# Seven block products in two more feed-forwards of a two-model kernel, and modulation units moved into down projections

## The chip, the cores and the metric

One core of one Trainium2 chip runs the whole program. The metric is the device time of one execution in microseconds (us); lower is better.

## The reference

Two models run one behind the other on 512 tokens of width 1024 (`D_MODEL`), in float32. The first has two layers, each a mixer and a SwiGLU feed-forward of width 2816; the second has one layer whose feed-forward has width 4096 and a squared ReLU. Shift, scale and gate of the first model's layers ("modulation") are one product of a condition vector with `ada_w` (1024 x 6144 in each layer).

```python
mod = cond @ ada_w[layer] + ada_b[layer]
sh1, sc1, g1, sh2, sc2, g2 = jnp.split(mod, 6, axis=-1)
...
h = modulate(rms_norm(x, ffn_norm[layer]), sh2, sc2)
x = x + g2[:, None, :] * swiglu(h, ffn_w1[layer], ffn_w2[layer])      # first model
...
u = jnp.square(jax.nn.relu(rms_norm_2(x, norm2_w) @ w_up))            # second model
return x + u @ w_down
```

## The kernel before, in words

Activations lie with features on the 128 partitions and the 512 tokens (`S`) along the free axis. Weights come as units of 128 x 1024 floats (512 KB), one for each 128 output features and 1024 inputs, from one long array `in_stream`. SyncE fills a ring of four (`ring`); GpSimd splits each unit into an upper half rounded to fp32r (`uppers`) and the rest (`lowers`, in the ring's own place). A plain product of one 128 x 128 weight block is three matmuls of 512 columns (upper by high, upper by low, lower by high; `products`), so a unit is 24 matmuls, here called a tile. Everything waits by semaphores, each engine runs its own program in order, and the order is written out by hand.

The stages are called m0 and f0 (mixer and feed-forward of layer 0), n1, m1 and f1 (layer 1), and f2 (feed-forward of the second model).

- **f0 before** (`ffn`): 44 up tiles in eleven rounds of four (gate, up, gate, up), the first round on the raw input before its norm is known, then 8 down tiles of 22 chunks each. VectorE multiplies gate by up, splits the result and writes it to `hid`.
- **f1 before** (`ffn1`): three plain rounds of four tiles, then 16 pairs of a gate and an up unit by **seven products**. A pair is seen as a 2 x 2 matrix of blocks (two units by two halves of the inputs) and the activations as 2 x 2 (halves of the inputs by halves of the tokens). Seven block products on sums of them (`seven_products`) take the place of eight: each is 4 x 3 matmuls of 256 columns, a pair 84 of them in place of 48 matmuls of 512. The sums and their halves are made beside it: VectorE `t_sum` and `t_lower`, ScalarE `t_upper`, `gate_uppers` and `up_uppers`, GpSimd one difference and four `lowers`; between products ScalarE copies partial results out of PSUM (`snaps`) and VectorE adds them back (`sums`). Since the sums need room, the hidden rows are kept only eight chunks at a time (`hid1`): the 22 chunks are taken in parts of 8, 8 and 6, each with its own down projection (`down_part`, stages f1a, f1b, f1c) and its own addition into the residual (`residual`).
- **f2 before**: two halves of 16 plain up tiles and 8 down tiles of 16 chunks.

**Modulation units.** `ada_w` is read in units of 128 x 1024, four to a group of 512 outputs. A unit is one DMA on ScalarE's queue into one of two buffers, and two multiply-adds of 128 x 512 on VectorE (`late_unit`, `ada_unit`); a group ends in `chunk_carry`, and TensorE sums it over the partitions with four small matmuls (`late_sum`, `ada_sum`), which wait until the fourth unit has been read. VectorE may overwrite `chunk_carry` only when that sum is done. Ten "late" groups are done in f0's up rounds: each round has one group, two units behind each pair, loaded into `sq` and `rs`. Four "last" groups are done in f0's down projection: VectorE takes group k ahead of `residual`'s chunk k, and TensorE sums group n-1 behind down tile n, for n = 1 to 4. TensorE may begin down tile n + 4 only when the residual of tile n has drained its bank.

Behind f0, `residual` with `held` makes the raw halves for n1 (`raw_split`, VectorE) for seven of eight chunks in one go, ahead of the last residual.

Of the kernel before, what the change touches and what calls it, by code (L numbers as in the profile page):

```python
# [38 lines left out]
P = 128  # L39
D = 1024  # L40
KC = D // P
# [97 lines left out]
def build(nc, A, plan):  # L139

    ctx = ExitStack()
    with ctx:
# [47 lines left out]
        late_w = [sq, rs]  # L190
# [27 lines left out]
        HIDDEN_AT = {"f0": 0, "f1": FF}  # L218
# [14 lines left out]

        PARTS = (KC, KC, FF - 2 * KC)
        HEAD = 2
        PLAIN = 3
# [63 lines left out]
        last_w = [big[:, TAIL + n * UNIT:TAIL + (n + 1) * UNIT].rearrange("p (a b) -> p a b", b=S) for n in (1, 2)]  # L300
# [105 lines left out]
        def _(pe):  # L406
# [370 lines left out]
            def late_sum(i):  # L777

                pe.wait_ge(sem("late_read1"), i * 2 + 2)
                for c in range(NT):  # L780
                    mm = pe.matmul(ps[:, 7, bass.ds(i * NT + c, 1)], C("chunk_carry")[:, c * P:(c + 1) * P],
                                   ones[:, 0:1], start=True, stop=True, skip_group_check=True)
                mm.then_inc(sem("late_sum_free"), 1)

            def ffn(st, layer):
                stream(f"w1_{layer}", 0, 2 * FF)
                slot = ring_loop(FF // 2, 4)
                take = bank_loop(FF // 2, range(4), [(st, "up", q) for q in range(4)])
                for q in range(4):
                    take(0, q)  # L790
                    raw_tile(st, q, q, slot(0, q), lambda k: (raw_hi[:, k, :], raw_lo[:, k, :]), True, loop["base"] + q)
                late_bank = nuse[7]
                uses["late"] = (7, late_bank)
                nuse[7] += 1
                with pe.Fori(1, FF // 2) as i:
                    for q in range(4):
                        take(i, q)
                        s = slot(i, q)
                        for k in range(KC):
                            if q == 0:  # L800
                                normed(st, k)
                            mm = products(ps[:, q, :], s, k, x_hi[:, k, :], x_lo[:, k, :], k == 0, k == KC - 1)
                        mm.then_inc(emptied[s], 1)
                    pe.wait_ge(drained[7], late_bank)
                    late_sum(i - 1)

                stream(f"w2_{layer}", 0, KC * FFU)
                slot = ring_loop(2, 4 * FFU)
                last_tile[st] = loop["base"] + (KC - 1) * FFU
                hidden = {FF - 2: (drained[1], nuse[1]), FF - 1: (drained[3], nuse[3])}  # L810
                take = bank_loop(2, range(4), [(st, "y", q) for q in range(4)], FFU)

                def down_tile(i, q):
                    take(i, q)
                    for f in range(FF):
                        if f % 8 == 0:
                            s = slot(i, FFU * q + f // 8)
                        if q == 0 and f in hidden:
                            pe.wait_ge(*hidden[f])
                        mm = products(ps[:, q, :], s, f % 8, hid[:, 0, f, :], hid[:, 1, f, :],  # L820
                                      f == 0, f == FF - 1)
                        if f % 8 == 7:
                            mm.then_inc(emptied[s], 1)
                    mm.then_inc(emptied[s], 1)

                for n in range(KC):
                    down_tile(n // 4, n % 4)
                    if 1 <= n <= ADA_LAST:
                        if n == 1:
                            claim(7, "late2", True)  # L830
                        ada_sum("last", n - 1, C("chunk_carry"), ps[:, 7, (n - 1) * NT:n * NT])
# [61 lines left out]
            def down_part(st, pack, part):  # L893
# [7 lines left out]
                with pe.Fori(0, 2) as i:  # L901
                    for q in range(4):
# [12 lines left out]
                        mm.then_inc(emptied[s], 1)  # L915

            def ffn1(st):

                stream("w1_1", 0, 2 * KC)
                slot = ring_loop(PLAIN, 4)  # L920
                take = bank_loop(PLAIN, range(4), [(st, "up", q) for q in range(4)])
                for q in range(4):
                    take(0, q)
                    raw_tile(st, q, q, slot(0, q), raw1, True, loop["base"] + q)
# [10 lines left out]
                down_part("f1a", "w2_1", 0)  # L935
                stream("w1_1", 2 * KC, 2 * KC)
                seven_products(st, KC)
                down_part("f1b", "w2_1", 1)
                stream("w1_1", 4 * KC, 2 * PARTS[2])
                seven_products(st, PARTS[2])  # L940
                claim(7, "meta_ss")
                pe.wait_ge(sem("meta_squared"), 1)
                for k in range(KC):
                    mm = pe.matmul(ps[:, 7, 0:META], ones[:, :], sq[:, 0, k * META:(k + 1) * META],
                                   start=k == 0, stop=k == KC - 1)
                mm.then_inc(full[7], 1)
                down_part("f1c", "w2_1", 2)
# [253 lines left out]
            ffn("f0", 0)  # L1201


            def late_raw(k):
                return late_hi[:, k, :], late_lo[:, k, :]

            stream("cd", 0, 4)
            raw_tiles("n1", [("u", t) for t in range(4)], late_raw, True)
# [13 lines left out]
            ffn1("f1")  # L1222
# [192 lines left out]
            for half in range(2):  # L1415
                st = f"f2{half}"
                stream("up2", half * HALF2, HALF2)
                slot = ring_loop(HALF2 // 4, 4)
                take = bank_loop(HALF2 // 4, range(4), [(st, "up", q) for q in range(4)])
                if half == 0:  # L1420
                    for q in range(4):
                        take(0, q)
                        raw_tile("f2", q, q, slot(0, q), x_halves, False)
                with pe.Fori(1 - half, HALF2 // 4) as i:
                    for q in range(4):
                        take(i, q)
                        s = slot(i, q)
                        for k in range(KC):
                            mm = products(ps[:, q, :], s, k, x_hi[:, k, :], x_lo[:, k, :], k == 0, k == KC - 1)
                        mm.then_inc(emptied[s], 1)  # L1430
                stream("down2", half * KC * 2, KC * 2)
                slot = ring_loop(2, 8)
                hidden = {HALF2 - 4 + b: (drained[b], nuse[b]) for b in range(4)}
                take = bank_loop(2, range(4), [(st, "y", q) for q in range(4)], 2)
                with pe.Fori(0, 2) as i:
                    for q in range(4):
                        take(i, q)
                        for f in range(HALF2):
                            if f % 8 == 0:
                                s = slot(i, 2 * q + f // 8)  # L1440
                            if q == 0 and f in hidden:
                                pe.wait_ge(*hidden[f])
# [56 lines left out]
        def _(act):  # L1499
# [66 lines left out]
            def ffn(st):  # L1566
                for m in range(2):
                    late_load(m, m)
# [1766 lines left out]
```

## Time and profile before

| | |
|---|---|
| median of 3 runs | 2526.47 us (2524.81 to 2528.64) |
| the profiled execution | 2526.73 us, its span 2524.7 us |
| PE busy | 2465.2 us, 98% of the span |
| POOL, DVE, ACT busy | 1787.9, 1144.8, 542.3 us |
| moved by DMA | 267.64 MB, mean 106 GB/s |
| mean granted TensorE clock | 0.992 |

In the profile PE is TensorE, DVE is VectorE, ACT is ScalarE, POOL is GpSimd, SP is SyncE; `ACTq` is ScalarE's sequencer, which issues its DMAs. A row names a line of the kernel, the engine, and output and inputs by the program's tile names. A matmul's duration is modelled and overlaps the next one's, so its pace is read from the distance of the starts.

### The profile page before, as it was taken

The page shows a single profiled execution, that of the slowest core. Times are in us where ns is not written, and L with a number is a line of the kernel's source. Part 1 is how long each engine was busy: PE and PEld are TensorE (multiplying, and loading weights), DVE is VectorE, ACT ScalarE, POOL GpSimd, SP SyncE. Part 2 cuts the span into 40 slices and gives each one's busy share as a digit, 9 for nine tenths or more (in the row PEclk, how much of TensorE's full clock was granted, in tenths as well). Part 3 has the DMA queues.
Part 4 walks back from the last instruction along what each step waited for, and adds up shares of the span by engine and source line. Part 5 has one row for each costly group of instructions (what it writes and reads, how often), then busy time and mean ns, then how long its engine had stood idle before and what let it go on. Part 6 is the DMA issues. An engine that isn't in the chain of part 4 may idle for free.

```text
span 2524.7 us, 34103 instructions
## 1 busy us (share of the span) xinstructions
PE 2465.2 (98%) x12183; PEld 1997.5 (79%) x12183; DVE 1144.8 (45%) x2070; ACT 542.3 (21%) x1091; POOL 1787.9 (71%) x1519
## 2 busy tenths in 40 slices
PE   6999999999999999999999999999999999999998
PEld 3677778888887768898988778788878888888886
DVE  5897756444337448363570223105664124331322
ACT  3213520000012522151511011113443101100100
POOL 5564367788887457767798755786555988888885
PEclk9999999999999999999999999999999999999999
DMA  6323225555532122232342211221112222222222
GB/s 260 125 75 134 75 100 178 188 182 173 195 104 75 47 68 92 99 109 93 107 159 97 84 59 59 84 92 67 59 51 101 93 98 92 93 98 100 92 100 83
DMA packets 73376, 267.64 MB, mean 106 GB/s; under 512 B 8240, under 2 KB 9024, under 8 KB 72768
## 3 DMA queue, kind: packets, MB, share of 16 engines
q1 hardware_dynamic: 60288, 215.97, 25.3%
q10 hardware_dynamic: 12992, 50.34, 5.8%
q8 instruction: 67, 1.10, 0.2%
q14 instruction: 29, 0.24, 0.0%
HBM read 262.08 MB, written 4.19 MB: 105 GB/s over the span
## 4 chain that ended last, share of the span: by engine, by line
PE 88%; DVE 6%; POOL 2%; ACT 1%; DMA 1%; issue 1%; ACTq 0%; DVEq 0%; SPq 0%; POOLq 0%
PE ps L444 22%; PE ps L445 22%; PE ps L446 22%; PE ps L845 2%; PE ps L849 2%; PE ps L848 2%; PE ps L675 2%; PE ps L676 2%; PE ps L677 2%; PE ps L1278 1%; PE ps L696 1%; PE ps L1334 1%; POOL lowers L2195 1%; DMA ring<-in_stream 1%; PE ps L1359 1%
## 5 line engine op out<-in xcount | busy, mean ns | idle before, releaser
L2192 POOL TENSOR_TENSOR uppers<-ring,ones 128x512 fp32r<-128x512 f32 x714 | 758.2, 1062 | 562.6 <-DMA ring<-in_stream 558.6
L2195 POOL TENSOR_TENSOR lowers<-ring,uppers 128x512 fp32r<-128x512 f32 x714 | 937.9, 1314 | 55.9
L444 PE MATMUL ps<-x_hi,uppers 128*128 128x512 f32 x864 | 351.5, 407 | 0.0
L446 PE MATMUL ps<-x_hi,lowers 128*128 128x512 f32 x864 | 337.3, 390 | 0.0
L445 PE MATMUL ps<-x_lo,uppers 128*128 128x512 f32 x864 | 337.0, 390 | 0.0
L444 PE MATMUL ps<-h_hi,uppers 128*128 128x264 f32 (+1 forms) x832 | 285.7, 343 | 4.0 <-DVE od_lo L3146 3.4
L445 PE MATMUL ps<-h_lo,uppers 128*128 128x264 f32 (+1 forms) x832 | 279.6, 336 | 0.0
L446 PE MATMUL ps<-h_hi,lowers 128*128 128x264 f32 (+1 forms) x832 | 278.8, 335 | 0.0
L445 PE MATMUL ps<-hid,uppers 128*128 128x512 f32 x704 | 274.3, 390 | 0.0
L444 PE MATMUL ps<-hid,uppers 128*128 128x512 f32 x672 | 263.0, 391 | 0.0
L446 PE MATMUL ps<-hid,lowers 128*128 128x512 f32 x672 | 261.6, 389 | 0.0
L1509 ACT ACTIVATE gate<-ps 128x512 f32<-128x512 f32 (+3 forms) x136 | 72.8, 536 | 731.1 <-PE ps L446 536.9
L444 PEld LDWEIGHTS ps<-x_hi,uppers 128*128 128x128 f32 x864 | 162.7, 188 | 42.6 <-issue 10.3
L445 PEld LDWEIGHTS ps<-x_lo,uppers 128*128 128x128 f32 x864 | 162.7, 188 | 38.6 <-issue 6.5
L446 PEld LDWEIGHTS ps<-x_hi,lowers 128*128 128x128 f32 x864 | 162.5, 188 | 34.8
L444 PEld LDWEIGHTS ps<-h_hi,uppers 128*128 128x128 f32 x832 | 157.2, 189 | 31.9 <-issue 8.8
L445 PEld LDWEIGHTS ps<-h_lo,uppers 128*128 128x128 f32 x832 | 157.2, 189 | 17.6 <-issue 0.7
L446 PEld LDWEIGHTS ps<-h_hi,lowers 128*128 128x128 f32 x832 | 157.1, 189 | 16.4
L445 PEld LDWEIGHTS ps<-hid,uppers 128*128 128x128 f32 x704 | 132.5, 188 | 27.7 <-issue 0.7
L1509 ACT ACTIVATE big<-ps 128x512 f32<-128x512 f32 (+7 forms) x151 | 68.0, 470 | 375.0 <-PE ps L446 184.8
L444 PEld LDWEIGHTS ps<-hid,uppers 128*128 128x128 f32 x672 | 126.2, 188 | 26.5 <-issue 0.5
L446 PEld LDWEIGHTS ps<-hid,lowers 128*128 128x128 f32 x672 | 126.1, 188 | 26.4
(432 smaller groups left out, 4180.9 us busy)
## 6 DMA issues: line engine op xcount, KB each, us to landing
ring<-in_stream SPq DMA_DIRECT2D x389, 512.0 KB, 3.2
sq<-in_ada_late ACTq DMA_DIRECT2D x20, 512.0 KB, 3.2
rs<-in_ada_late ACTq DMA_DIRECT2D x20, 512.0 KB, 4.7
big<-in_ada_late ACTq DMA_DIRECT2D x16, 512.0 KB, 4.3
big<-in_stream SPq DMA_DIRECT2D x13, 512.0 KB, 16.0
gate<-in_ada_rest ACTq DMA_DIRECT2D x12, 512.0 KB, 3.2
big<-in_ada_rest ACTq DMA_DIRECT2D x12, 512.0 KB, 3.8
hbuf<-in_stream SPq DMA_DIRECT2D x4, 512.0 KB, 6.8
```

The source lines that it names most:

```text
L444: pe.matmul(out, upper, hi, start=start, stop=False)
L445: pe.matmul(out, upper, lo, start=False, stop=False)
L446: return pe.matmul(out, lower, hi, start=False, stop=stop)
L675: pe.matmul(out, hi[:, at], upper, start=k == 0, stop=False)
L676: pe.matmul(out, hi[:, at], lower, start=False, stop=False)
L677: mm = pe.matmul(out, lo[:, at], upper, start=False, stop=k == KC - 1)
L845: mm = pe.matmul(out, upper[:, at], hi[:, k, :], start=start and k == 0, stop=False, skip_group_check=True)
L848: pe.matmul(out, upper[:, at], lo[:, k, :], start=False, stop=False, skip_group_check=True)
L849: mm = pe.matmul(out, lower[:, at], hi[:, k, :], start=False, stop=k == HALF_K - 1, skip_group_check=True)
L1509: return act.activation(out, in_, func, **kw)
L2192: pool.tensor_tensor(uppers[:, s, at], w[:, at], ones[:, 0:1].broadcast_to((P, UNIT // 2)), ALU.mult)\
L2195: pool.tensor_tensor(lowers[:, s, at], w[:, at], uppers[:, s, at].bitcast(F32), ALU.subtract)\
```

## The change

f0 now takes the way of f1, with its own ranges of units: three plain rounds, 2, 8 and 6 pairs by seven products, and three down parts (f0a, f0b, f0c). The modulation groups leave the up rounds. Late groups 0 to 4 go to f0a and 5 to 9 to f0b: VectorE does them between the residual's chunks, TensorE sums them behind down tiles 1, 2, 4, 5 and 6, and ScalarE issues their loads when its own part of the up run is done. The last four groups stay with the final down projection, which now is f0c with 6 chunks to a tile. The two load buffers are those of the last groups for all.

f2 takes two plain rounds (8 tiles), then 12 pairs by seven products, four to a run, each pair two up tiles with the squared ReLU (`wide_step`), and four down parts of 8 chunks.

```diff
-        late_w = [sq, rs]
...
+        LATE_GROUPS = ((0, 1), (2, 3, 4), (5, 6, 7, 8, 9))
+        LATE_SUM_BEHIND = (1, 2, 4, 5, 6)
...
+            def late_behind(n, first):
+
+                if n in LATE_SUM_BEHIND:
+                    late_sum(first + LATE_SUM_BEHIND.index(n))
+
+            def last_behind(n):
+
+                if 1 <= n <= ADA_LAST:
+                    if n == 1:
+                        claim(7, "late2", True)
+                    ada_sum("last", n - 1, C("chunk_carry"), ps[:, 7, (n - 1) * NT:n * NT])
...
+                down_part(st + "a", w2, 0, early)
...
+                down_part(st + "b", w2, 1, late)
...
+                down_part(st + "c", w2, 2, last)
...
+            def late_loads(first, count):
+
+                for unit in range(first, first + count):
+                    if unit >= 2:
+                        act.wait_ge(sem(f"late_read{unit % 2}"), unit // 2)
+                    late_load(unit, unit % 2)
+
...
                 for run in (1, 2):
+                    if st == "f0":
+                        late_loads(5 * ADA_UNITS * (run - 1), 5 * ADA_UNITS)
                     first_weights(st, run)
                     seven_run(st, run, 0)
...
+            def early_groups(k):
+
+                if k == 0:
+                    late_group(0)
+                    late_group(1)
+                    late_out(0)
+                elif 3 <= k < 6:
+                    late_group(k - 1)
+                elif k == 6:
+                    late_out(1)
+
+            def late_groups(k):
+
+                if k in (0, 1, 2, 4, 5):
+                    late_group(5 + (0, 1, 2, 4, 5).index(k))
+                elif k == 6:
+                    late_out(2)
...
-            residual("m0", "f0", 0, 2, raw=lambda k: (raw_hi[:, k, :], raw_lo[:, k, :]))
-            ffn("f0")
+            residual("m0", "f0", 0, 2, raw=raw0)
+            ffn1("f0", 0)
...
-            residual("f0", "n1", 0, 5, raw=lambda k: (late_hi[:, k, :], late_lo[:, k, :]), held=last_tile["f0"], last=True)
+            residual("f0c", "n1", 0, 5, raw=late0, held=True, last=True)
```

`late_out` waits on VectorE for the sums of the groups so far and adds the bias. ScalarE's step of a pair in f2 is that of f1 with these operations of its own:

```diff
+                act.wait_ge(sem("sums"), after(i, 10, 5 * (c + HEAD) + 3))
+                f(sq[:, 0, :], ps[:, 6, :], ACT.Relu).then_inc(sem("f2_relu"), 1)
+                act.wait_ge(sem("products"), after(i, 14, 7 * (c + HEAD) + 7))
+                f(gate[:, e, H:S], ps[:, 2 * e, 0:H], ACT.Relu).then_inc(sem("snaps"), 1)
+                act.wait_ge(sem("snaps"), after(i, 10, 5 * (c + HEAD) + 4))
+                link(f(sq[:, 1, :], gate[:, e, :], ACT.Square))
+                f(hid1[:, 0, first, :], sq[:, 1:2, :], ACT.Copy).then_inc(sem("f2_upper_half"), 1)
+                act.wait_ge(sem("sums"), after(i, 10, 5 * (c + HEAD) + 4))
+                f(hid1[:, 0, second, :], ps[:, 6:7, :], ACT.Copy).then_inc(sem("snaps"), 1)
```

**Where the late units stand on VectorE.** Of before, in one round of f0's up loop: two units (`big` is not among their inputs, `sq` and `rs` are) stand behind one pair's product and split.

```order
L2596 TENSOR_TENSOR ps<-gate,ps 128x512 [waits emptied2]
...
L2598 COPY hid<-ps 128x512
...
L2600 TENSOR_TENSOR hid<-ps,hid 128x512
...
L2417 TENSOR_SCALAR ps<-sq,cond 128x512 [waits late_filled0]
...
L2424 SCALAR_TENSOR_TENSOR ps<-sq,cond,ps 128x512 [waits late_half]
L2424 SCALAR_TENSOR_TENSOR ps<-rs,cond,ps 128x512 [waits late_read0,late_filled1]
```

Of the change, from the last step of f0's first up run to the first residual of f0a; `late_filled` is a landed unit, L2401 is the residual.

```order
L2538 TENSOR_TENSOR hid_62<-ps,hid_62 128x512 [waits snaps]
L2472 TENSOR_SCALAR ps<-big,cond 128x512 [waits late_filled0]
...
L2479 SCALAR_TENSOR_TENSOR ps<-big,cond,ps 128x512 [waits late_read0,late_filled1]
...
L2479 SCALAR_TENSOR_TENSOR consts<-big,cond,ps 128x512 [waits late_sum_free,late_half]
L2587 TENSOR_TENSOR mod<-ps,vecs 128x8 [waits late_sum_free]
L2401 SCALAR_TENSOR_TENSOR xres<-ps,mod,xres 128x512 [waits emptied1,drained7]
```

Before, two units stood behind each pair; now eight stand in a row with nothing between them, and twenty in each of f0a and f0b.

**Where TensorE waits for them.** Of the change, the end of tile 1 of f0a, the sum of late group 0 (L798), and the start of tile 2.

```order
L461 MATMUL ps<-hid_62,lowers 128x512
L798 MATMUL ps<-ones,consts 128x1 [waits late_read1,drained7]
L798 MATMUL ps<-ones,consts 128x1 x3
L459 MATMUL ps<-hid_62,uppers 128x512 [waits lower_made3,snaps,drained2]
L460 MATMUL ps<-hid_62,uppers 128x512
```

The sum stood behind four up tiles before, a whole round after the group's first load; now it stands behind the second down tile, with all of the part's later tiles queued behind it.

**Where the loads start on ScalarE.** Of the change, from ScalarE's last step of the first up run to the first loads.

```order
L1508 ACTIVATE gate<-ps 128x256 [waits products]
L1508 ACTIVATE hid1_62<-ps 128x512 [waits sums]
L1563 DMA big<-in_ada_late 128x1024 x2
L1563 DMA big<-in_ada_late 128x1024 [waits late_read0]
L1563 DMA big<-in_ada_late 128x1024 [waits late_read1]
```

The first two loads follow the run's last copy, and each later one waits until the unit two before it has been read.

## Rows read from the trace of the kernel before

**Rows 1.** The page: busy time; the chain that ended last, by engine.
```profile
PE 2465.2 (98%) x12183; PEld 1997.5 (79%) x12183; DVE 1144.8 (45%) x2070; ACT 542.3 (21%) x1091; POOL 1787.9 (71%) x1519
...
PE 88%; DVE 6%; POOL 2%; ACT 1%; DMA 1%; issue 1%; ACTq 0%; DVEq 0%; SPq 0%; POOLq 0%
```

**Rows 2.** Windows, PE alone: start:end, length, PE busy, clock, DMA share, GB/s.
```profile
389.30:616.40 227.10, 227.10 (x1042) 1.00 0.55 185
616.40:740.00 123.60, 123.60 (x562) 1.00 0.48 162
964.60:1008.20 43.60, 43.60 (x193) 1.00 0.29 97
1008.20:1029.30 21.10, 20.45 (x169) 1.00 0.29 101
1072.90:1154.10 81.20, 80.83 (x673) 1.00 0.31 104
1197.70:1258.80 61.10, 60.68 (x506) 1.00 0.31 103
```

**Rows 3.** PE's timeline: a late sum in f0; starts of two pairs in f1.
```profile
411.15 0.95 PE L781 MATMUL ps<-ones,consts 128*128 128x1 f32 x8
...
1093.62 0.28 PE L845 MATMUL ps<-x_hi,uppers 128*128 128x256 f32 x1
...
1103.70 0.28 PE L845 MATMUL ps<-x_hi,uppers 128*128 128x256 f32 x1
```

**Rows 4.** VectorE's timeline: the first group of four units in f0's down projection.
```profile
620.24 0.74 DVE L2394 TENSOR_SCALAR ps<-big,cond 128x512 f32<-128x512 f32 x1
...
625.45 1.55 DVE L2396 SCALAR_TENSOR_TENSOR ps<-big,cond,ps 128x512 f32<-128x512 f32 x2 [2.09 <-DMA big<-in_ada_late]
...
629.49 0.75 DVE L2400 SCALAR_TENSOR_TENSOR consts<-big,cond,ps 128x512 f32<-128x512 f32 x1
```

**Rows 5.** DMA issues of the page: KB each, median us to landing.
```profile
sq<-in_ada_late ACTq DMA_DIRECT2D x20, 512.0 KB, 3.2
...
big<-in_ada_late ACTq DMA_DIRECT2D x16, 512.0 KB, 4.3
```

**Rows 6.** Timeline of the next group: issues, then the two landings.
```profile
635.37 1.92 ACTq L1700 DMA_DIRECT2D big<-in_ada_late  x2
...
638.60 1.55 DVE L2396 SCALAR_TENSOR_TENSOR ps<-big,cond,ps 128x512 f32<-128x512 f32 x2 [1.67 <-DMA big<-in_ada_late]
642.22 0.76 DVE L2396 SCALAR_TENSOR_TENSOR ps<-big,cond,ps 128x512 f32<-128x512 f32 x1 [2.07 <-DMA big<-in_ada_late]
```

**Rows 7.** ScalarE's timeline: its last step of f1's first up run.
```profile
1030.72 0.60 ACT L1509 ACTIVATE hid<-ps 128x512 fp32r<-128x512 f32 x1 [0.83 <-DVE ps L2481]
```

**Rows 8.** VectorE's timeline: end of f0's down projection.
```profile
725.25 0.75 DVE L2348 SCALAR_TENSOR_TENSOR xres<-ps,mod,xres 128x512 f32<-128x512 f32 x1 [12.74 <-PE ps L446]
...
730.69 0.69 DVE L2307 CAST hid<-ps 128x512 fp32r<-128x512 f32 x1 [3.30 <-PE ps L446]
...
740.21 0.75 DVE L2348 SCALAR_TENSOR_TENSOR xres<-ps,mod,xres 128x512 f32<-128x512 f32 x1 [0.16 <-PE ps L446]
...
742.97 0.69 DVE L2308 TENSOR_TENSOR hid<-ps,hid 128x512 fp32r<-128x512 f32 x1
```

**Rows 9.** Windows, PE alone, around a wait of TensorE ahead of f1.
```profile
929.80:933.80 4.00, 0.04 (x2) 0.78 0.38 133
933.80:938.80 5.00, 5.00 (x20) 0.50 0.01 3
```

**Rows 10.** Timelines of ScalarE and VectorE between two pairs of f1.
```profile
1105.15 0.60 ACT L1509 ACTIVATE hid<-ps 128x512 f32 x1 [0.86 <-DVE ps L2481]
1105.64 0.38 ACT L1509 ACTIVATE rs<-ps 128x256 f32<-128x256 f32 x1
...
1106.61 0.69 DVE L2439 TENSOR_TENSOR ps<-ring 128x512 f32<-128x512 f32 x1
1107.21 0.42 DVE L2465 TENSOR_TENSOR gate<-ps,rs 128x256 f32<-128x256 f32 x1
```

More of the change, by code:

```diff
@@ L783, in late_sum @@
                 mm.then_inc(sem("late_sum_free"), 1)
[L785 to L831, printed above, removed]
@@ L900, in down_part, with tile @@
                 done = state["pairs"]
-                with pe.Fori(0, 2) as i:
-                    for q in range(4):
+                def tile(i, q, first=True):
                         take(i, q)
@@ L1412, in _, with wide_part @@
             mix_out("m2", "w_out2", lambda k: (od_hi[:, k, :], od_lo[:, k, 0:S]))
[L1415 to L1434, printed above, removed]
+            def wide_part(seg):
+                st = f"f2{seg}"
+                for t in range(KC):
+                    stream("down2", (seg // 2) * 2 * KC + 2 * t + seg % 2, 1)
+                slot = ring_loop(2, 4)
+                plain = {KC - 4 + b: (drained[b], nuse[b]) for b in range(4)}
+                take = bank_loop(2, range(4), [(st, "y", q) for q in range(4)])
+                done = state["pairs"]
                 with pe.Fori(0, 2) as i:
@@ L2321, in sum_square, with residual @@
                 ins.then_inc(sem("x_summed"), 1)
-            def residual(y, st, layer=None, part=0, raw=None, held=None, rs2=False, last=False, between=None):
+            def residual(y, st, layer=None, part=0, raw=None, held=False, rs2=False, last=False, between=None, before=None):
                 for k in range(KC):
+                    if before is not None:
+                        before(k)
                     if between is not None and k == KC - 1:
@@ new lines, in wide_sums @@
+            def wide_sums():
+                early, late = half_tokens_at
+                near, far, other = ps[:, 5, :], ps[:, 4, :], sq[:, 1, 0:H]
+                for k in range(HALF_K):
+                    dve.wait_ge(sem("sum_copy"), 8 * list(runs).index("f2") + k + 1)
+                    s2, s1, s3, s4 = (s_sum[:, n, k, :] for n in range(4))
+                    tt(s3, near[:, early], other, ALU.subtract)
+                    link(tt(s1, far[:, late], other, ALU.add))
+                    link(tt(s2, s1, near[:, early], ALU.subtract))
+                    tt(s4, far[:, early], s2, ALU.subtract).then_inc(sem("sum_input"), 1)
+                dve.memset(small[:, 10:11], 0.0).then_inc(sem("sum_input"), 1)
@@ L3208, in _ @@
+            wide_sums()
+            plain_squares(0)
+            sums_lowers("f2")
+            plain_squares(1)
+            dve.wait_ge(sem("x_root"), 2 * NORMS["f2"] + 2)
+            for run in range(3):
+                residual(f"f2{run}", None, rs2=True, between=lambda: first_weights("f2", run))
+                wide_run(run)
+            residual("f23", "nf", rs2=True)
             dve.wait_ge(sem("final_root"), 1)
```

307 lines of the change are left out of this document (197 added, 110 removed).

## The prediction

> **What bounds the kernel now.** I read the page first: PE is busy for 98% of the span and 88% of the chain that ended last is PE [rows 1]. So time is gained only by taking columns from TensorE, and lost wherever TensorE waits in its program order. Then the windows by stage [rows 2]: f0's up rounds and its down projection have PE busy without a gap at full clock, 227.1 and 123.6 us, and f1, which already works by seven products, shows what such runs take: 2, 8 and 6 pairs in 21.1, 81.2 and 61.1 us, and the eight plain tiles ahead of them in 43.6 us. Last I read VectorE's and ScalarE's timelines where the modulation units are done behind f0's up rounds [rows 4 to 6], since the change moves forty of them under TensorE's waits.
>
> **The change, part by part.**
>
> *Columns.* A plain tile takes 43.6 / 8 = 5.45 us, so a plain pair 10.9 us; a pair by seven products starts every 1103.70 - 1093.62 = 10.08 us [rows 2, 3], 0.82 us less. Run by run f1 needs 0.9, 0.6 and 0.6 us more than its pairs times 10.08, about 0.7 at each start.
>
> - f0 before: 227.1 + 123.6 = 350.7 us from the second up round to the end of the down projection [rows 2]. After, if nothing waits: 43.6 (plain) + 21.1 + 81.2 + 61.1 (runs) + 16 down tiles at 5.45 = 87.2 + 8 down tiles of six chunks at 4.09 = 32.7 + 14 sums at 0.95 [rows 3] = 13.3; together 340.2. The sums are the same fourteen as before. **Gain 10.5 us.**
> - f2: 12 x 0.82 - 3 x 0.7 = **7.7 us gained.**
>
> *The step of f2 on ScalarE and VectorE.* No row shows it. Against f1's, ScalarE has two ReLU, a square and one copy of 512 more where f1 has one activation, and VectorE one subtraction more. In f1 ScalarE takes up the hidden copy at 1105.15 and the snapshot that the third product of the next pair needs at 1105.64; VectorE takes up the sum that the fourth product needs at 1107.21 and has it at 1107.63, while that product begins 3 x 10.08 / 7 = 4.32 us after its pair, at 1108.02 [rows 3, 10]. In f2 the first ReLU fits where ScalarE idles, the square and two copies end some 0.3 us later than f1's copy, and VectorE's last subtraction some 0.15 us later, so the slack of 0.39 us shrinks to 0.25. Bounds: nothing, or 0.3 us lost in each of 12 pairs = 3.6. I take **0**, the nearer end by these rows.
>
> *The units' pace.* A unit is 1.55 us on VectorE, but the first group of four in f0's down projection takes 620.24 to 630.24, **10.0 us**, with VectorE waiting for each unit beyond the two preloaded [rows 4]. Two buffers, each loaded only when read: two units take one load and 1.55 us. A load alone lands in 3.2 us, the median of this place is 4.3 [rows 5]; the two issued at 635.37 and some 1.6 later landed at 638.60 and 642.22 [rows 6], 3.2 and 5.3 us. That gives 2.4 to 3.4 us a unit, 2.95 at the median. In f0a and f0b the ring's loads come less often, since TensorE waits, so I take T = **2.8 us**, between the lone load and the median. In the up rounds these units had 5.7 us each (227.1 / 40), so nobody waited for them; in f0a and f0b twenty stand against 43.6 + 5 x 0.95 = 48.3 us of TensorE's work, and in f0c sixteen against 32.7 + 4 x 0.95 = 36.5 us.
>
> *Where it is paid.* Times from the first matmul of a down part. f1's first run ends on ScalarE at 1030.72, 1.4 us behind TensorE's end of the run at 1029.3 [rows 2, 7]; two loads go out behind it at about 2.1, the first lands at 5.3, the group is read at 5.3 + 10.0 = 15.3. TensorE has tile 1 done at 10.9, waits 4.4, sums, and each later sum waits for its own group:
>
> - f0a: twenty units end at 15.3 + 16 x 2.8 + 1.0 (VectorE waits for the second sum in `late_out`, ahead of all residuals) = 61.1; sum 0.95 and tile 7, 5.45, end at 67.5. **19.2 us lost.**
> - f0b: the same count and, tile 3 and 4 apart, the same waits: **19.2 us lost.**
> - f0c: VectorE's coefficients take it to about 5.0, so the load still sets the start. Sixteen units end at 15.3 + 12 x 2.8 + 0.5 (residual and square sum between groups, mostly under the loads) = 49.4; the sum and tiles 5, 6, 7 (12.3) end at 62.6. Against 36.5: **26.1 us lost.**
>
> *The raw halves for n1.* Before, seven splits began at 730.69 during a last tile of 15 us, and the last residual at 740.21 found its tile just done [rows 8]. They take 9.4 us. Now the last tile lasts 4.1 us. From the end of tile 6: residual at 0.2, splits 2.4 to 11.8, last residual 11.9, its split ready 2.8 later, by 742.97 + 0.69 less 740.21 = 3.45, at 15.3. TensorE could have its first raw tile done at 12.7 and has it at 16.5. **3.8 us lost.**
>
> *The clock.* Ahead of f1 PE waits 4.0 us, then works 5.0 us at a granted 0.50, which is 1.2 GHz, then at 2.4 again [rows 9]: 2.5 us of work lost. Waits of 4 to 7 us stand behind five tiles in f0a, four in f0b and four in f0c. Where the next sum waits for VectorE anyway a slow tile is hidden (5.45 + 2.5 + 0.95 is less than the group's 11.2). It shows where nothing follows: tile 7 in f0a and f0b, tiles 5 to 7 in f0c. 3 x 2.5 = **7.5 us**; bounds 0 and 15 (six exposed).
>
> The Trainium skill's page "TensorE: Matmul & The Clock Gate" (section "HAM oscillation — how this bites in real kernels") says that matmul bursts parted by waits for DMA start each one at the half clock; by it every one of the thirteen bursts here would start slow. Taken with all of them on the path it would add 13 x 2.5 = 32 us instead of 7.5, and the sum would be 2609; the trace of before has only lone waits and can't show a row of them.
>
> **The sum**, against the profiled execution's 2526.7 (0.2 above the median of 2526.47): 2526.7 - 10.5 - 7.7 + 19.2 + 19.2 + 26.1 + 3.8 + 7.5 = **2584.3 us**, +2.3%. In T the three parts hold 16 + 16 + 12 = 44 T: at 2.4 the sum is 2567, at 3.4 it is 2611.
>
> **Rivals.**
>
> 1. *Lone-load pace.* With TensorE waiting, few ring loads collide, T falls to 2.4: 2584 - 17.6 = 2567; with little half clock 2562. For it: the 3.2 us of [rows 5, 6]. Against: two unit loads still overlap each other.
> 2. *The half clock reaches the path* in most bursts, as a mechanism of this kernel: tiles 3 and 4 of f0a and f0b, which have no sum between them, and the starts of the runs behind them go slowly too: + 4 x 2.5 = 2594, up to 2600 with T at 2.95.
> 3. *Ring and units crowd each other*, T = 3.2 or more: 2602 and up. For it: 5.3 us of the second load in [rows 6]. Against: the median of 4.3.
> 4. *The other side: the units hide and the columns decide.* If TensorE never waited for a group the time would be 2526.7 - 18.2 = 2508.5. It turns on one thing, the pace of a unit: the losses without the clock are 44 T - 54.9, and equal the gain of 18.2 at T = 1.66. VectorE alone needs 1.55, so the loads would have to be hidden almost wholly; that they are not is what the three DMA waits of [rows 4, 6] show.
> 5. *f2 stalls in every pair*: + 3.6, 2588; inside the range.
>
> **How the numbers follow.** Chances: my forecast with its own range 2573 to 2593, 0.50; rival 1 0.20; rival 2 0.14; rival 3 0.11; rival 4, or the change with a part of it, 0.03; rest 0.02. The predicted time is that of the forecast, 2584. The range for 8 in 10 leaves out the far end of rivals 1 and 3 and all of 4: 2563 to 2605. A measurement of this kernel tells 0.2%, 5 us, from no change. Faster 0.03, same 0.01, slower 0.96.
>
> **What the profile of the changed kernel would show.** Right: TensorE's pairs in f0 and f2 start every 10.1 us; TensorE's idle rows at the late and last sums name VectorE's multiply-add, 4 to 5 us each in f0a and f0b, 6 to 7 in f0c; VectorE's rows between them name the DMA of `in_ada_late`; f0a and f0b take 66 to 70 us each and f0c 61 to 66; granted clock of the down parts below 0.9; f2 takes 8 us less than before; all other stages stand as they were. Wrong: a unit's pace near 1.6 us; late sums without idle time; a half clock in the windows of the runs (rival 2); PE waiting for ScalarE or VectorE once in each pair of f2.

## The result, and the profile after

The changed kernel takes **2590.57 us** (median of 4 runs, 2586.48 to 2591.14) against 2526.42 of the kernel before beside it (2524.81 to 2528.64): ratio 1.0249, 95% interval 1.0237 to 1.0261, slower. The forecast was 2584 in a range from 2563 to 2605. The profiled execution took 2590.53 us, with a span of 2588.5.

The page of the changed kernel, busy time and the chain by engine, against [rows 1]:

```profile
PE 2478.6 (96%) x13191; PEld 2050.1 (79%) x13191; DVE 1331.1 (51%) x2371; ACT 725.2 (28%) x1475; POOL 1715.1 (66%) x1435
...
PE 78%; DVE 9%; DMA 6%; issue 3%; POOL 2%; ACT 2%; ACTq 0%; DVEq 0%; SPq 0%; POOLq 0%
```

TensorE's share of the chain that ended last fell from 88% to 78%; VectorE, DMA and idle time without a visible cause (`issue`) took most of what it lost. The windows by stage show where: start:end, length, PE busy, granted clock, DMA share, GB/s. In order: f0's plain tiles, run 0, f0a, run 1, f0b, run 2, f0c, n1's first tiles; then four of f2's stages.

```profile
390.30:433.90 43.60, 43.60 (x193) 1.00 0.30 97
433.90:454.80 20.90, 20.40 (x169) 1.00 0.35 102
454.80:526.40 71.60, 59.40 (x234) 0.83 0.61 206
526.40:608.50 82.10, 80.98 (x674) 1.00 0.32 103
608.50:676.50 68.00, 58.31 (x234) 0.85 0.63 216
676.50:738.20 61.70, 61.03 (x506) 1.00 0.33 102
738.20:804.70 66.50, 47.96 (x178) 0.79 0.57 190
804.70:837.00 32.30, 30.30 (x140) 0.95 0.23 74
2231.70:2277.00 45.30, 45.30 (x197) 1.00 0.30 93
2277.00:2320.60 43.60, 43.60 (x194) 1.00 0.31 97
2320.60:2362.20 41.60, 40.87 (x338) 1.00 0.32 102
...
2490.80:2532.10 41.30, 40.79 (x337) 1.00 0.34 103
```

The runs of pairs take what f1's take within 1 us [rows 2]. The three down parts do not: 71.6, 68.0 and 66.5 us stand against the 48.3, 48.3 and 36.5 of TensorE's own work, 73.0 us more in all. f0 from its second round to the end of the down projection takes 804.7 - 390.3 = 414.4 us for 350.7 before, 63.7 more, which is the whole difference of the spans (63.8); n1's 3.7 more, f2's 6.0 less (344.0 for 350.0) and 2.3 more elsewhere cancel.

TensorE's waits in the three parts (us in total, times, longest), and VectorE's timeline at the start of f0a, against [rows 4]:

```profile
PE ps L798 <- DVE consts L2479: 21.9, 8, 3.8
PE ps L750 <- DVE consts L2453: 17.4, 4, 7.6
```

```profile
459.79 0.75 DVE L2472 TENSOR_SCALAR ps<-big,cond 128x512 f32<-128x512 f32 x1 [2.23 <-DMA big<-in_ada_late]
460.57 2.40 DVE L2479 SCALAR_TENSOR_TENSOR ps<-big,cond,ps 128x512 f32<-128x512 f32 x3
466.21 2.40 DVE L2479 SCALAR_TENSOR_TENSOR ps<-big,cond,ps 128x512 f32<-128x512 f32 x3 [3.23 <-DMA big<-in_ada_late]
468.65 0.75 DVE L2479 SCALAR_TENSOR_TENSOR consts<-big,cond,ps 128x512 f32<-128x512 f32 x1
```

The sums on TensorE (line 798 in f0a and f0b, line 750 in f0c) wait for the multiply-add that closes a group, and the first group's third unit waits 3.23 us for a load issued only when the first unit had been read. f0a's first group is read 14.6 us into the part. The closing multiply-adds of f0a's first and fifth groups start at 468.65 and 516.48, four groups of four units apart: (516.48 - 468.65) / 16 = 2.99 us a unit; in the same way f0b has 2.88 and f0c 2.82. These paces include what else VectorE does between the groups.

### The profile page after: what moved, and what is told of

Same layout as the page of the kernel before. It is cut to its first block, busy times and chain, and to the rows that moved or that the text cites. A ratio compares the mean times of both kernels' runs of the same rounds, so it can differ in the third digit from the quotient of the medians.

```text
span 2588.5 us, 37060 instructions
## 1 busy us (share of the span) xinstructions
PE 2478.6 (96%) x13191; PEld 2050.1 (79%) x13191; DVE 1331.1 (51%) x2371; ACT 725.2 (28%) x1475; POOL 1715.1 (66%) x1435
## 4 chain that ended last, share of the span: by engine, by line
PE 78%; DVE 9%; DMA 6%; issue 3%; POOL 2%; ACT 2%; ACTq 0%; DVEq 0%; SPq 0%; POOLq 0%
PE ps L459 16%; PE ps L460 16%; PE ps L461 16%; PE ps L814 5%; PE ps L818 5%; PE ps L817 5%; DMA big<-in_ada_late 4%; PE ps L690 2%; PE ps L691 2%; PE ps L692 2%; DMA ring<-in_stream 2%; PE ps L1267 1%; DVE ps L2479 1%; PE ps L711 1%; PE ps L1323 1%
## 5 line engine op out<-in xcount | busy, mean ns | idle before, releaser
L2244 POOL TENSOR_TENSOR uppers<-ring,ones 128x512 fp32r<-128x512 f32 x602 | 645.1, 1072 | 556.6 <-DMA ring<-in_stream 553.0
L2247 POOL TENSOR_TENSOR lowers<-ring,uppers 128x512 fp32r<-128x512 f32 x602 | 799.5, 1328 | 47.2
L461 PE MATMUL ps<-hid,lowers 128*128 128x512 f32 x672 | 270.4, 402 | 0.0
L2273 POOL TENSOR_TENSOR lowers<-ring,uppers 128x512 fp32r<-128x512 f32 x176 | 222.9, 1302 | 0.0
L2284 POOL TENSOR_TENSOR ring<-ring 128x512 f32<-128x512 f32 x44 | 57.0, 1295 | 221.1 <-DVE ps L2494 221.1
L1508 ACT ACTIVATE big<-ps 128x512 f32<-128x512 f32 (+7 forms) x179 | 78.7, 456 | 382.5 <-PE ps L461 184.8
L459 PE MATMUL ps<-x_hi,uppers 128*128 128x512 f32 x416 | 176.5, 424 | 0.0
L1508 ACT ACTIVATE uppers<-ring 128x512 fp32r<-128x512 f32 x176 | 101.4, 632 | 259.2 <-DMA ring<-in_stream 151.7
L461 PE MATMUL ps<-x_hi,lowers 128*128 128x512 f32 x416 | 163.1, 392 | 0.0
L460 PE MATMUL ps<-x_lo,uppers 128*128 128x512 f32 x416 | 162.9, 392 | 0.0
L1508 ACT ACTIVATE gate<-ps 128x512 f32<-128x512 f32 (+3 forms) x124 | 59.4, 482 | 325.5 <-PE ps L461 179.0
```

What stands on the lines that cost most here:

```text
L459: pe.matmul(out, upper, hi, start=start, stop=False)
L460: pe.matmul(out, upper, lo, start=False, stop=False)
L461: return pe.matmul(out, lower, hi, start=False, stop=stop)
L1508: return act.activation(out, in_, func, **kw)
L2244: pool.tensor_tensor(uppers[:, s, at], w[:, at], ones[:, 0:1].broadcast_to((P, UNIT // 2)), ALU.mult)\
L2247: pool.tensor_tensor(lowers[:, s, at], w[:, at], uppers[:, s, at].bitcast(F32), ALU.subtract)\
```

## The experiments

Each kernel starts from the changed one unless said otherwise, and each set ran on one chip with the kernel before. The ratios are against that.

**The two halves of the change apart.** `e1_f2_only` is the kernel before with the new f2; `e2_f0_only` the changed kernel with the old f2.

> The first model's feed-forward as it was before, the second model's with three runs of four pairs, as in the change. My theory: the whole loss of the change is in f0, and f2 is a gain of its own, 6.0 us by the two traces (344.0 against 350.0 us), so 2526.4 - 6.0 = 2520.4 us, with f2's runs at 41.5 us each. Rival, that f2's gain depends on what f0 left behind it, or is within what the runs can tell: 2525 to 2527.

> The first feed-forward as in the change, the second model's as before. If the two parts of the change are independent: 2590.6 + 6.0 = 2596.6 us. Rival, that the two interact: a sum of the two parts' effects that misses the change's own 64.1 by more than 2 us.

With f2 alone: 2522.4 us (11 runs) against 2527.8, ratio 0.9981 (0.9972 to 0.9990), 5.4 us faster: the one version here that beats both kernels. With f0 alone: 2600.4 us (4 runs, 2593.1 to 2600.6), ratio 1.0278 (1.0262 to 1.0295), 72.6 us slower. The two differences add to 67.2 us. The change as a whole came to 64.1, 61.6 and 66.7 us in three sets. The sum misses the 64.1 by 3.1, more than the 2 us that the rival named, but no more than the three sets differ among themselves, so no interaction is shown. Windows of f2's plain tiles and three runs in `e1_f2_only`:

```profile
2163.50:2208.80 45.30, 45.30 (x197) 1.00 0.28 93
2252.30:2293.70 41.40, 40.85 (x337) 1.00 0.32 103
2337.30:2378.80 41.50, 40.93 (x338) 1.00 0.32 102
2422.30:2463.90 41.60, 40.91 (x338) 1.00 0.32 102
```

f2 lasts 2163.5 to 2507.5, 344.0 us, as in the changed kernel.

**The loads taken away.** 52 of the 56 loads are left out, those of the last groups too; VectorE's arithmetic and its order stay.

```diff
-                    if unit >= 2:
-                        act.wait_ge(sem(f"late_read{unit % 2}"), unit // 2)
-                    late_load(unit, unit % 2)
+                    if unit < 2:
+                        late_load(unit, unit % 2)
...
-                dve.wait_ge(sem(f"late_filled{m}"), i * 32 + 16 * (j // 2 + 1))
+                if i == 0 and j < 2:
+                    dve.wait_ge(sem(f"late_filled{m}"), 16)
```

> The changed kernel, but only 4 of the 56 modulation units are loaded; all others multiply what their buffer holds, so the modulation values are not the reference's. VectorE's instructions and their order are unchanged. My theory, that a unit's pace is set by its load, which is issued only when the buffer before last was read: the pace falls from the 2.88 us of the trace to the two multiplications' own 1.6, and by the formula of the prediction (losses of the three down parts 44 T - 54.9, and no time at half clock) 15.5 of the 73 us lost stay: 2533 us. Rival, that VectorE's own work and its order cost the time (units ahead of the residual adds that empty the banks): over 2580.

Measured: 2530.8 us (10 runs), ratio 1.0013 (1.0003 to 1.0022). The windows of f0a, f0b and f0c in its trace:

```profile
456.90:505.80 48.90, 48.53 (x234) 1.00 0.34 108
...
587.40:635.80 48.40, 48.40 (x235) 1.00 0.27 87
...
697.40:747.00 49.60, 42.94 (x177) 0.86 0.34 106
```

Some 60 of the 64 us hang on the loads. In f0a and f0b next to nothing is left of the loss. The window of f0c stops short: its last matmul starts at 747.20, and n1's first at 748.65 behind a wait of 1.07 us for GpSimd's `lowers`. Counted to there, like the 66.5 above, f0c takes 51.3 us where TensorE needs 36.5, and TensorE's waits name the unit's multiply-add:

```profile
PE ps L750 <- DVE consts L2451: 6.7, 4, 3.2
```

So the rival, VectorE's own work and order, holds a share: 14.8 us in f0c, the step to n1 included. There VectorE closes a group every 8.5 us, residual and squares among them, while TensorE has one tile of 4.1 us and a sum to do. The granted clock is 0.86 in this window, and that costs little: the second and the fourth sum wait only 0.18 and 0.20 us, since slow tiles fill the time that the first and the third spend waiting (3.09 and 3.19). The 2533 expected was met with a pace that was too low: a unit took 1.86, 1.80 and 2.12 us for 1.6, but the first groups were read 11.3, 8.9 and 11.3 us into their parts, not 15.3.

**Four buffers instead of two.** The load then goes out two units earlier. The last groups' loads and their waits, not shown, change in the same way, and two steps of later stages count on other semaphores.

```diff
-        late_w = last_w = [big[:, TAIL + n * UNIT:TAIL + (n + 1) * UNIT].rearrange("p (a b) -> p a b", b=S) for n in (1, 2)]
+        NB = 4
+        late_w = last_w = [big[:, at:at + UNIT].rearrange("p (a b) -> p a b", b=S)
+                           for at in (TAIL + UNIT, TAIL + 2 * UNIT, AFTER_UPPERS + 8 * S, AFTER_UPPERS + 10 * S)]
...
-                    if unit >= 2:
-                        act.wait_ge(sem(f"late_read{unit % 2}"), unit // 2)
-                    late_load(unit, unit % 2)
+                    if unit >= NB:
+                        act.wait_ge(sem(f"late_read{unit % NB}"), 2 * (unit // NB))
+                    late_load(unit, unit % NB)
```

> Four buffers for the units' loads instead of two (the two new ones in the area of the columns' lower halves, which the down parts don't use); the loads are issued two units earlier. My theory, that a unit's pace of 2.88 us is a load's issue and latency behind a read buffer, not a rate: pace 1.8, between the 1.5 of the multiplications and the 2.2 at which units and columns together would take what 206 GB/s at a DMA share of 0.61 comes to at a full share (338 GB/s). By the formula of the losses (44 T - 54.9 = 24.3 of the 73 stay) 2542 us; at 2.0 us it is 2550. Rival, that the rate of the transfers sets the pace already: over 2575.

Measured: 2543.8 us (5 runs, 2539.8 to 2545.7), ratio 1.0068 (1.0055 to 1.0082); 45 us of the loss are gone. Its windows of f0a, f0b and f0c (the last one again stops short; to n1's first matmul at 757.68 it is 52.5 us), and its waits in them:

```profile
456.80:509.00 52.20, 49.00 (x233) 1.00 0.77 282
...
591.00:643.90 52.90, 50.43 (x235) 0.97 0.78 278
...
705.20:756.00 50.80, 42.54 (x176) 0.87 0.71 249
```

```profile
PE ps L755 <- DVE consts L2462: 8.3, 4, 3.2
PE ps L803 <- DVE consts L2487: 5.7, 5, 1.9
```

And the page's row of the loads (KB each, median us to landing), here and in the changed kernel:

```profile
big<-in_ada_late ACTq DMA_DIRECT2D x56, 512.0 KB, 5.5
```

```profile
big<-in_ada_late ACTq DMA_DIRECT2D x56, 512.0 KB, 4.0
```

One load takes longer, 5.5 us for 4.0, and yet a unit takes less: counted between the same multiply-adds 2.13, 2.04 and 2.22 us in the three parts, for 2.99, 2.88 and 2.82. So the pace was a latency between reading a buffer and its next landing, not a rate: the two-buffer kernel moved 206 GB/s in f0a, this one 282. Without loads VectorE itself needed 1.86, 1.80 and 2.12 us a unit in the same count, so with four buffers it is nearly VectorE's own pace.

The forecast of 2542 was met by two errors that cancelled. My pace of 1.8 us was too low. And the losses at a given pace were too high: the first group of f0a is read 11.7 us into the part, of f0b and f0c 11.6 and 11.3, together 11.3 earlier than three times the 15.3 in the formula's constant; and the constant -54.9 holds n1's 3.8, which the 73.0 us do not. Down parts alone, it gives 16 x 2.13 + 16 x 2.04 + 12 x 2.22 - 58.7 - 11.3 = 23.4 us. The trace has 52.2 + 52.9 + 52.5 - 133.1 = 24.5, of which 1.1 is the step from the last tile to n1.

The Trainium skill's page "Trainium Kernel Development and Optimization" (section "Best Practices") advises double buffering, to overlap transfers with work. Here two buffers overlap too little: two units of work are 3.1 us and a load lands in 4.0.

**The first loads earlier.** Only the start of each part is changed: its first two loads go out ahead of the run before it, or, where the two buffers are still in use, as soon as they are read.

```diff
+                if st == "f0":
+                    late_loads(0, 2)
                 seven_run(st, 0, 2 * PLAIN)
                 for run in (1, 2):
                     if st == "f0":
-                        late_loads(5 * ADA_UNITS * (run - 1), 5 * ADA_UNITS)
+                        late_loads(5 * ADA_UNITS * (run - 1) + 2, 5 * ADA_UNITS - 2)
                     first_weights(st, run)
+                    if st == "f0" and run == 1:
+                        late_loads(5 * ADA_UNITS, 2)
+                    if st == "f0" and run == 2:
+                        for m in range(2):
+                            act.wait_ge(sem(f"late_read{m}"), 2 * ADA_LATE)
+                            last_load(m)
                     seven_run(st, run, 0)
...
```

> The first two loads of each of the three down parts are issued ahead of the run of up pairs before the part (f0c's two in ScalarE's order ahead of run 2), not at its start. The first unit of a part starts 5.0 us into it in the trace (f0a) with the load issued at the part's start. Theory of the load's latency: each part is shorter by 2 to 2.5 us, 6 to 7 us in all, 2584. Rival, that the pace of the later loads makes up for the start, or that ScalarE's waits at the runs' starts cost the same: no change, 2590.

> The changed kernel as it is, as the measure for the three others on one chip: 2590.6 us if the chips agree, up to 2595 if the two runs of the change's kernels so far above their own profiles (2593 to 2597 for the kernel with the fill, whose profiled execution took 2585.6) are a property of this program's executions and not of the fill.

`e5_prefetch` took 2591.1 us (5 runs, 2586.4 to 2595.4), the changed kernel beside it 2589.0 (2587.3 to 2597.2): ratios 1.0246 (1.0232 to 1.0260) and 1.0243 (1.0229 to 1.0257). No gain. The first group of f0a was read 1.3 us earlier into its part than in the kernel beside it (13.5 us for 14.8), where 2 to 2.5 were expected. In f0b and f0c it was read 13.7 and 15.7 us in; the changed kernel had 13.8 and 15.8 in its first trace. And the start of run 1 lost time. VectorE's first column sum of run 1, in this kernel and then in the changed one beside it:

```profile
531.93 0.70 DVE L2497 TENSOR_TENSOR ps<-ring 128x512 f32<-128x512 f32 x1 [4.21 <-DMA ring<-in_stream]
```

```profile
537.43 0.70 DVE L2494 TENSOR_TENSOR ps<-ring 128x512 f32<-128x512 f32 x1 [3.51 <-DMA ring<-in_stream]
```

It waits for the ring's load, 0.7 us longer with two more loads under way. TensorE then waits 1.77 us for VectorE, the granted clock is 0.65 from 534.8 to 538.8, and the run takes 84.2 us for 82.0 in the kernel beside it.

**TensorE kept busy in its waits.** Matmuls into an idle bank ahead of the waiting sums; their results are read by nobody. `e4_fill` has 22 more of them ahead of each sum in f0c; the other two have none there.

```diff
+            def fill(n):
+
+                for _ in range(n):
+                    pe.matmul(ps[:, 6, :], hid1[:, 1, 0, 0:P], hid1[:, 0, 0, :], start=True, stop=True)
...
+                fill(0 if i in (2, 7) else 14)
                 pe.wait_ge(sem("late_read1"), i * 2 + 2)
```

> The changed kernel with matmuls into an idle bank ahead of the sums on which TensorE waits (14 ahead of each sum in f0a and f0b but two, 22 ahead of each in f0c), which fill its waits of 3 to 8 us and are read by nobody. Theory of the prediction: the half clock after these waits costs some 7.9 us in the parts' ends and 0.9 at the next run's start, and the fill gives it back: 2582 us, granted clock over 0.95 in all three parts. Rival, that VectorE's pace hides the half clock everywhere: 2590, though the clock is up. Against both: the fill outlasts waits, up to 2600.

> The fill of matmuls into an idle bank ahead of the sums in f0a and f0b alone (14 each, but groups 2 and 7), none in f0c, where the profile of the kernel with 22 showed no gain. Theory, that the half clock after TensorE's waits costs time in these two parts: by that kernel's profile (f0a 68.2 against 71.6, f0b 65.1 against 68.0) 6.3 us less than the changed kernel beside it, 2584. Rival, that the pace of the loads decides and the fill only takes the idle time: the same time as the changed kernel, within 2 us.

> The fill ahead of the sums of f0a and f0b once more. In its profile the ends of the two parts (last sum to the run's first product) were 7.4 and 6.5 us, against 9.1 and 8.1 in the changed kernel's, and run 1 lost nothing: if the half clock costs what these ends show, the time is 3 to 5 us under the changed kernel's beside it, 2586. Rival, that what the half clock costs is given back or hidden by the pace of the loads: ten executions of each together agree within 2 us.

> The changed kernel once more, beside the kernel with the fill on one chip, since five executions of each spread over 10 us: a median of 2588 to 2592 us again.

Medians: `e4_fill` 2595.3 (4 runs, ratio 1.0270, 1.0254 to 1.0285), and its trace has 68.8 us in f0c for 66.5, so the 22 are too many there; `e4b_fill_late` 2590.9 (ratio 1.0255, 1.0241 to 1.0269) beside 2589.0; `e4c_fill_late_2` 2590.7 (ratio 1.0256, 1.0242 to 1.0270) beside 2593.2 (ratio 1.0257, 1.0243 to 1.0271), 1.2 above the 2588 to 2592 expected of it. Ten executions of each, fill in f0a and f0b or none, have means of 2590.6 and 2591.2. By the times the rival holds. The traces tell another thing. f0a to run 2 with the fill (`e4b_fill_late`), then without (`e0_after_again`):

```profile
456.70:524.10 67.40, 63.27 (x290) 0.97 0.65 218
524.10:606.20 82.10, 81.16 (x674) 1.00 0.34 103
606.20:671.80 65.60, 63.27 (x290) 0.97 0.69 224
671.80:733.20 61.40, 60.80 (x506) 1.00 0.33 103
```

```profile
460.10:533.00 72.90, 60.04 (x235) 0.84 0.62 202
533.00:615.00 82.00, 80.93 (x673) 1.00 0.32 103
615.00:684.20 69.20, 56.30 (x235) 0.88 0.63 213
684.20:745.40 61.20, 60.68 (x505) 1.00 0.34 103
```

These four stretches take 276.5, 279.5 and 276.7 us in the three profiled executions with the fill, and 283.4, 285.3 and 286.5 in the three of the changed kernel; `e2_f0_only` and `e7_raw_early`, with the same four stretches and no fill, have 284.8 and 281.7. The other executions of the same kernels do not repeat that: eight with the fill have a mean of 2591.5, eight without 2590.1. Each of the three profiled executions with the fill was also the fastest of its kernel, so they do not stand for the rest. Why is open.

**The raw halves for n1 earlier.** VectorE makes those of tiles 0 to 4 ahead of residual 5, not ahead of residual 7; ScalarE's order follows.

```diff
-                    if k == KC - 1 and held:
-                        for n in range(KC - 1):
+                    if k == ADA_LAST + 1 and held:
+                        for n in range(ADA_LAST + 1):
                             raw_split(st, n, *raw(n))
...
-                    if raw is not None and (not held or k == KC - 1):
+                    if raw is not None and (not held or k > ADA_LAST):
```

> The changed kernel with the raw halves of tiles 0 to 4 made ahead of the residual addition of tile 4's successor, and not ahead of the last tile's. The trace has 32.3 us in the first stage behind f0c for 28.6 before, 3.7 more. My theory, that VectorE's five halves stand between the last down tile and the first product behind it: 3.7 us less than the changed kernel beside it, 2586. Rival, that the halves then push the last groups' residual additions out and nothing is gained: the same within 2 us.

> Four buffers for the units' loads and the raw halves earlier, both together. By my theory of the raw halves 2543.8 - 3.7 = 2540 us; by its rival 2544. Neither brings f0 under the kernel before: the kernel without loads, with no wait left for one, still took 2530.8.

`e7_raw_early`: 2593.2 us (5 runs, 2592.0 to 2595.8), ratio 1.0265 (1.0251 to 1.0279), beside 2593.2: nothing gained. `e8_four_raw`: 2548.4 us (4 runs, 2547.1 to 2551.7), ratio 1.0091 (1.0075 to 1.0106), where four buffers alone had 1.0068 (1.0055 to 1.0082) in another set: nothing gained, and by the medians some 5 us lost. My remedy was wrong. In `e8_four_raw`, VectorE's sum of tile 6's squares, and TensorE's first instruction for n1:

```profile
761.65 0.68 DVE L2379 TENSOR_TENSOR big<-ps,sq 128x512 f32<-128x512 f32 x1
```

```profile
762.54 0.37 PE L505 MATMUL ps<-uppers,shift_halves 128*2 128x256 f32 x1 [6.60 <-issue]
```

TensorE's program waits for these sums before n1's first tile (the wait on `x_summed` in `raw_tile`, line 520 of the changed kernel), and the halves now stood ahead of them: TensorE idles 6.60 us. In the changed kernel the sum comes first (800.97), and the delay sits further on. VectorE's last residual, and TensorE's row for the last tile's squares, against the row at 740.21 of [rows 8]:

```profile
810.83 0.74 DVE L2401 SCALAR_TENSOR_TENSOR xres<-ps,mod,xres 128x512 f32<-128x512 f32 x1
```

```profile
812.29 1.38 PE L491 MATMUL ps<-sq,ones 128*128 128x512 f32 x2 [1.99 <-ACT sq L1508]
```

The seven pairs of splits (801.58 to 810.83) keep the last residual back, the last tile's square waits for it, and TensorE for the square. No run moved the splits without moving them ahead of something else, so what a better order would give is not shown.

## Why the prediction was right

The time, the sign, the place and the mechanism were right: TensorE waits in program order for groups whose pace the loads set. Term by term, predicted and measured in the profiled execution:

- **Columns**, f0 gains 10.5. Holds within 1.3: plain tiles 43.6, runs 20.9 + 82.1 + 61.7 = 164.7 for 163.4 forecast, down parts without load waits 48.9 and 48.4 for 48.3.
- **f2's gain**, 7.7: measured 6.0 by the trace, 5.4 by the times. The first pair of a run took 1.0, 0.9 and 0.8 us more than 10.08 where 0.7 was taken, and "I take 0" for the step of f2 was slightly short. ScalarE's snapshot and the third product that needs it, in the changed kernel:

```profile
2344.07 0.38 ACT L1508 ACTIVATE rs<-ps 128x256 f32<-128x256 f32 x1
```

```profile
2344.30 0.28 PE L814 MATMUL ps<-x_hi,uppers 128*128 128x256 f32 x1
...
2344.69 0.35 PE L814 MATMUL ps<-s_hi,t_hi 128*128 128x256 f32 x1
```

  ScalarE's copy is due while the second product ends, and the third begins just behind it, 0.1 us late; pairs start 10.18 us apart (2331.60, 2341.78) for f1's 10.08. That the copy is the cause is read from these rows, no run tested it. The rest is the fourth product at a run's start, which waits 0.7, 0.6 and 0.5 us for VectorE's gate in the three runs. Rival 5, 3.6 us, did not come.
- **The pace**, T = 2.8: 2.99, 2.88, 2.82. They hold VectorE's work between the groups, which the sum had apart as 1.0, 1.0 and 0.5; without it they are 2.93, 2.82 and 2.78. **The first group** at 15.3: 14.6, 13.8, 15.8. The last group of the three parts was to be read 171.6 us into them in all, and is at 172.0. `e3_no_loads` and `e6_four_buffers` show that the latency of two buffers makes the pace. Rivals 1 and 3 (2.4 and 3.2) fall. One reading behind rival 1 was too kind: the 3.2 us of [rows 5] are not of a load alone, but of the first of two issued close together. The second took 4.7, in a row of the page of the kernel before that [rows 5] leaves out:

```profile
rs<-in_ada_late ACTq DMA_DIRECT2D x20, 512.0 KB, 4.7
```

- **f0a, f0b, f0c** with the clock 70.0, 70.0 and 65.1: 71.6, 68.0 and 66.5. f0 as a whole 412.2: 414.4. The waits named as a sign were too long: 4 to 5 us each were expected in f0a and f0b, 6 to 7 in f0c, and 2.0 to 3.8, 1.4 to 3.0 and 2.5 to 7.6 came, since slow tiles fill part of the time.
- **The raw halves**, 3.8: n1's first stage took 3.7 more (32.3 for 28.6), but that number is partly chance. TensorE waits 1.99 us for the last square, and in this trace the half clock follows:

```profile
812.70:816.70 4.00, 4.00 (x11) 0.57 0.20 65
```

  In three other traces (`e0_after_again`, `e3_no_loads`, `e6_four_buffers`) the clock stayed at 1.00 behind the same wait, and the stage took 30.8 or 30.9 us: 2.3 more than before, not 3.7. To the term belongs, too, the step from f0c's last tile to n1, 1.3 us longer than before, in which TensorE waits 1.15 us for GpSimd's `lowers` (804.71): the splits on VectorE set when the last square comes, so an earlier start of n1 would only have made the later wait longer. Together 3.6. The mechanism, the last residual behind the splits, is read from the rows above; the experiment that should have shown it moved the splits ahead of something worse.
- **The clock**, 7.5. The parts' ends, from the last sum to the next stage, are 9.1, 8.1 and 16.7 us for 6.4, 6.4 and 13.2 at full clock: 7.9. Of these 1.3 are the step to n1, so the clock has 6.6 there, and 1.5 more in n1. TensorE at f0a's end:

```profile
517.28 1.87 PE L798 MATMUL ps<-ones,consts 128*128 128x1 f32 x8 [3.77 <-DVE consts L2479]
519.01 0.77 PE L459 MATMUL ps<-hid,uppers 128*128 128x512 f32 x1
...
526.40 0.28 PE L814 MATMUL ps<-x_hi,uppers 128*128 128x256 f32 x1
```

  Each of TensorE's waits in the down parts, twelve where thirteen were expected, is followed by a stretch at 1.2 GHz, at once or within 2.3 us, and the parts' granted clocks are 0.83, 0.85 and 0.79. By the Trainium skill's rule ("TensorE: Matmul & The Clock Gate", "HAM oscillation — how this bites in real kernels") bursts parted by waits for DMA each start slow. As to the bursts the trace agrees. As to the time, the 2609 that the prediction worked out with all bursts on the path did not come: TensorE is busy 165.7 us in the three parts for 133.1 at full clock, 32.6 more, but only 6.6 of it lie in the ends; the rest took the place of waiting, since the next group was not there any sooner. That the half clock costs the whole kernel some 8 us is only half shown: filling the waits shortened three profiled executions by some 7 us and no median. This term stays open.
- **The sum**: 2584.3 for 2590.5. Of the 6.2 us, 2.2 lie in f0, 1.7 in f2, and 2.3 before f0 and between n1 and f2, where I had taken the stages as unchanged. All three have the same sign; nothing large cancelled.
- **Rival 4**, units hidden: it turned on a pace of 1.66. `e3_no_loads`, with no load to wait for and 1.86 and 1.80 a unit in f0a and f0b, hid them there and came within 0.13% of the kernel before, not under it: f0c still loses 14.8 us and n1 takes 2.3 more (30.8 for 28.6), about what the columns give. Half its mechanism was right; this kernel, with no load left to wait for, did not come near the 2508.5.

## What to carry to other kernels

When a helper's transfers move from a long stretch into a short one, compare their pace with the stretch. One unit takes at least (landing time plus use) divided by the number of buffers, here (4.0 + 1.55) / 2 = 2.8 us with two, where 2.8 to 3.0 were measured; with four it is 1.8, where 2.0 to 2.2 were measured because VectorE's own pace is near that. With small work per load two buffers are bound by latency, not by bandwidth. Removing columns from TensorE pays only where nothing else becomes its program-order wait; split a change by stage before judging it, as f2's half was a gain and f0's a loss more than ten times as large. Before work is moved ahead on an engine, list what then stands behind it: here the squares' sums, on which TensorE's whole next stage waited.

## What the runs showed of the hardware

- Loads of 512 KB, median to landing: with up to two under way 4.0 us and 206 GB/s in all in f0a at a DMA share of 0.61, with up to four 5.5 us and 282 GB/s at a share of 0.77.
- In the changed kernel's f0a, four waits of TensorE of 3.66, 2.80, 1.96 and 3.77 us were each followed by work at 1.2 GHz. The length of one wait does not tell: in f0b the clock fell behind a wait of 1.38 us, while in the four-buffer kernel's f0a, with waits of 0.76, 1.89 and 0.55 us, and in n1's first stage behind waits of 2.1 and 2.2 us (`e0_after_again`, `e3_no_loads`, `e6_four_buffers`) it stayed at 1.00.
- By the trace of the changed kernel the half clock cost little: TensorE is busy 32.6 us more than at full clock in the three parts, and 6.6 us of it lie where no further wait follows.
- Single executions of the changed kernel spread over 11 us (2586.5 to 2597.2), those of the kernel before over 7 (2523.9 to 2531.0): f0a took 71.6, 72.9 and 71.5 us and f0b 68.0, 69.2 and 71.4 in its three traces. One profiled execution tells an effect of 5 us badly here.
